# The first RMS norm of x: sum of squares of the second tile on VectorE, both roots before both scalings

## The reference, cut to what matters

```python
def rmsnorm(x, g):
    xf = x.astype(jnp.float32)
    y = xf * lax.rsqrt(jnp.mean(xf * xf, axis=-1, keepdims=True) + EPS)
    return (y * g.astype(jnp.float32)).astype(x.dtype)

h = rmsnorm(x, ln_mix_g)
proj = h @ w_in            # 1024 -> [lru_x | lru_gate | q | k | v]
# ... recurrent branch, attention, output projection, cross-attention,
# ... a mixer over 128*128 experts (most of the time), final norm
```

## Time and profile before

| what | value |
|---|---|
| median of 3 runs | 969.2 us (968.04 to 970.23) |
| the profiled execution | 968.83 us |
| its span in the profile | 967.0 us |
| PE busy | 954.4 us (99%) |
| DVE busy | 806.9 us (83%) |
| ACT busy | 542.6 us (56%) |
| POOL busy | 486.4 us (50%) |

### The profile page before, as it was taken

One profiled execution on the slowest core, in us unless ns is written; L12 is line 12 of the kernel. 1 busy time (PEld: TensorE's weight loads), 2 busy tenths in 40 slices (PEclk: granted clock), 3 DMA queues, 4 the chain that ended last, 5 costly groups with the idle time before them and its releaser, 6 DMA issues.

```text
span 967.0 us, 18013 instructions
## 1 busy us (share of the span) xinstructions
PE 954.4 (99%) x6807; PEld 915.2 (95%) x6807; DVE 806.9 (83%) x1571; ACT 542.6 (56%) x953; POOL 486.4 (50%) x315
## 2 busy tenths in 40 slices
PE   8999999999999999999999999999999999999997
PEld 8897799999999999999998888889999999999997
DVE  5988866446999999999988787777899899999897
ACT  7775546555555546464465565545555455555456
POOL 1001001001488888888788888827478872242210
PEclk9999999999999999999999999999999999999999
DMA  9699865434547787878878878878999999999992
GB/s 317 218 316 323 269 226 200 147 123 139 175 82 203 180 208 179 213 169 205 202 189 208 194 174 194 201 202 307 329 362 345 338 347 374 361 372 354 366 339 95
DMA packets 134265, 235.61 MB, mean 244 GB/s; under 512 B 38624, under 2 KB 87520, under 8 KB 133824
## 3 DMA queue, kind: packets, MB, share of 16 engines
q1 hardware_dynamic: 97552, 208.66, 64.4%
q0 software_dynamic: 36224, 25.70, 14.1%
q10 hardware_dynamic: 432, 0.57, 0.2%
HBM read 216.38 MB, written 17.97 MB: 242 GB/s over the span
## 4 chain that ended last, share of the span: by engine, by line
PE 51%; POOL 33%; issue 8%; DVE 5%; ACT 2%; DMA 1%; ACTq 0%; POOLq 0%; DVEq 0%
POOL wmap L478 33%; PE acc L1702 11%; PE bank L1702 11%; PE acc L1438 11%; PE bank L1703 5%; PE acc L1703 5%; PE acc L1420 3%; DVE wsp L893 1%; PE acc L1421 1%; PE acc L1424 1%; ACT wsp L511 1%; PE bank L1544 1%; PE bank L1391 1%; DMA wmap<-gate,widx 1%; PE bank L1566 1%
## 5 line engine op out<-in xcount | busy, mean ns | idle before, releaser
L478 POOL DMA_INDIRECT wmap<-gate,widx x192 | 322.3, 1679 | 90.8 <-issue 60.0
L762 ACT ACTIVATE hl<-raw 128x1024 fp32r<-128x1024 f32 x192 | 202.3, 1058 | 80.3 <-PE bank L1668 41.7
L1143 DVE TENSOR_TENSOR hl<-raw,hl 128x1024 fp32r<-128x1024 f32 x99 | 120.9, 1221 | 24.2 <-ACT hl L762 24.1
L1635 PE MATMUL bank<-xt,hl 128*128 128x256 f32 x480 | 136.0, 283 | 0.0
L1636 PE MATMUL bank<-xt,hl 128*128 128x256 f32 x480 | 135.9, 283 | 0.0
L1637 PE MATMUL bank<-xt,hl 128*128 128x256 f32 x480 | 135.9, 283 | 0.0
L501 POOL DMA_INDIRECT vg<-v,idx_v x48 | 74.3, 1549 | 119.0 <-DVE acc_s L1284 99.7
L1150 DVE TENSOR_TENSOR hl<-raw,hl 128x512 fp32r<-128x512 f32 x186 | 119.3, 687 | 17.0 <-ACT hl L762 15.8
L1702 PE MATMUL bank<-whl,hl 128*128 128x416 f32 x380 | 121.1, 369 | 0.7 <-DVE acc L1292 0.7
L1702 PE MATMUL acc<-whl,hl 128*128 128x416 f32 x380 | 121.7, 371 | 0.0
L1667 PE MATMUL bank<-xt,hl 128*128 128x512 f32 x288 | 102.4, 399 | 0.0
(11 more groups left out here) (306 smaller groups left out, 2379.6 us busy)
## 6 DMA issues: line engine op xcount, KB each, us to landing
raw<-u_t SPq DMA_DIRECT2D x128, 512.0 KB, 4.5
raw<-v SPq DMA_DIRECT2D x128, 512.0 KB, 5.9
wmap<-zeros SPq DMA_DIRECT2D x6, 2048.0 KB, 11.7
wblk<-wmap SPq DMA_DIRECT2D x62, 192.0 KB, 6.1
wraw<-w_in SPq DMA_DIRECT2D x9, 1024.0 KB, 9.4
wraw<-w_pq SPq DMA_DIRECT2D x8, 1024.0 KB, 5.3
wraw<-w_ck SPq DMA_DIRECT2D x4, 1024.0 KB, 8.4
wraw<-w_cv SPq DMA_DIRECT2D x4, 1024.0 KB, 7.0
```

What stands on the lines that cost most here:

```text
L478: nc.gpsimd.indirect_dma_start(out=wmap, out_offset=bass.IndirectOffsetOnAxis(ap=set_ranks(widx, k)[:, h, r:r + 1], axis=0), in_=set_ranks ...
L762: nc.scalar.activation(eslot(k, 0, second), raw[:, k // 2, k % 2], ACT.Copy).then_inc(ready, 1)
L1143: V.tensor_tensor(eslot(k, 1, second), raw[:, k // 2, k % 2], eslot(k, 0, second).bitcast(F32), ALU.subtract).then_inc(ready, 1)
L1635: pe.matmul(dst, uh[:, c], xt[:, c, 0], start=(c == 0), stop=False)
```

## The change

ScalarE now squares and sums tile 0 alone. VectorE waits for tile 1 of x, squares and sums it itself (a `scalar_tensor_tensor` that computes (x*1)*x and has an accumulator output), then waits until both sums are there, makes both means, and after that does reciprocal and scaling of tile 0 and of tile 1. ScalarE takes both roots one after the other. The norms of other stages keep their order; `tile_norm` is only split into two functions.

```diff
             warm_sqrt()
+            act.wait_ge(s_x[0], 16)
+            squares(0, 0, xr, xs)
             for t in range(TT):
-                act.wait_ge(s_x[t], 16)
-                squares(0, t, xr, xs)
                 tile_deviation(0, t)
...
+                mean_square(n, t)
+                scale_tile(n, t, src, dst)
+
+            def mean_square(n, t):
+                ss = stat[:, SS + 2 * n + t:SS + 2 * n + t + 1]
                 V.tensor_scalar(ss, ss, 1.0 / D, EPS, ALU.mult, ALU.add).then_inc(s_var, 1)
+
+            def scale_tile(n, t, src, dst):
                 dve.wait_ge(s_std, norm_count(n, t))
...
             V.memset(stat[:, WARM:WARM + 1], 1.0).then_inc(s_warm, 1)
+            dve.wait_ge(s_x[1], 16)
+            V.scalar_tensor_tensor(xs[:, 1], xr[:, 1], 1.0, xr[:, 1], ALU.mult, ALU.mult,
+                                   accum_out=stat[:, SS + 1:SS + 2]).then_inc(s_sq, 1)
+            dve.wait_ge(s_sq, TT)
             for t in range(TT):
-                tile_norm(0, t, xr, xs)
+                mean_square(0, t)
+            for t in range(TT):
+                scale_tile(0, t, xr, xs)
```

## The result

| | before | changed |
|---|---|---|
| median, 22 runs each | 968.55 us | 970.78 us |
| lowest to highest | 966.95 to 970.25 | 967.84 to 974.95 |
| profiled execution, its span | 968.83, 967.0 us | 970.91, 969.1 us |

The ratio is 1.0025, with a 95% interval of 1.0014 to 1.0037: the change costs 2.2 us. The forecast was 970.1 us, a loss of 0.9 us, which it took for no change; the time lies in its range, the loss is more than twice the forecast one. The second row of that table already hints at the reason: the lowest of the changed kernel lies 0.9 us above the lowest of before, the highest 4.7 us above.

What follows compares the result with a forecast made beforehand. TensorE, busy for 99% of the span, was taken to bound the kernel, so a first projection 0.9 us later arrives whole at the end: 969.2 + 0.9 = 970.1 us, range 968.6 to 971.9, counted as no change.

Steps and rivals of the forecast that it cites:

- What bounds the kernel: TensorE, busy for 99% of the span: a later first projection shifts all behind it by as much, 0.9 us.
- Steps 1 to 4, the serial tail: First norm: tile 1's sum at 7.14, both scalings in a row on VectorE, second done at 9.39; plus 0.87 us.
- Step 5, TensorE: Tile 0's eight transposes run from 8.56 to 9.49, 0.93 us, and tile 1's follow: plus 0.93 us.
- The rival on the clock: TensorE, idle from 6.84 to 8.56, keeps the slow clock until the first projection: 2.8 us more, 972.9 us; chance 0.06.
- Half rate of the product: VectorE's accumulating product on tile 1 runs at half the rate: 1.22 us more, 971.4 us; chance 0.08.
- Slower by over 0.2%: Whole kernel: the case of a loss above 0.2%, from half rate, slow clock and scatter; chance 0.13.

Runs made afterwards that it cites:

- e5: The changed kernel as it is, run again beside a new set of before: 971.19 us, ratio 1.0022.
- e1: The changed kernel with 14 instead of 10 products on zeros ahead of the first transposes, filling TensorE's gap: 969.53 us, ratio 1.0006.
- e3: The kernel before with only the order changed: ScalarE squares both tiles, then both means, both roots, both scalings: 969.25 us, ratio 1.0014.
- e10: The changed kernel as it is, run again beside the one with 14 products on zeros (e9): 971.20 us, ratio 1.0019.
- e6: The changed kernel with 6 instead of 10 products on zeros, so that TensorE idles longer: 971.98 us, ratio 1.0032.
- e7: The kernel before with ScalarE taking the root straight from its own sum, no VectorE mean for these two tiles: 968.53 us, ratio 1.0002.
- e2: The kernel before with 7 instead of 10 products on zeros, nothing of the change: 969.59 us, ratio 1.0011.
- e9: The changed kernel with 14 instead of 10 products on zeros, as e1, now beside the changed kernel as it is (e10): 969.53 us, ratio 1.0003.

## Why the forecast was right and where it fell short

**The number.** That 970.78 us lies only 0.7 from the forecast 970.1 is partly luck. The forecast stood on 969.2 us, the median of three runs; in 22 runs the kernel before has 968.55. This hides 0.65 us of the 1.3 us by which the loss itself was missed.

**What bounds the kernel.** Right. The start of the expert pass (line 1635 of before, line 1648 now) follows the first projection: 278.2 us before, 280.5 with the change, 278.9 with the gap filled, 281.7 in e5.

```profile
L1635 PE MATMUL bank<-xt,hl x480: 278/283/382, 278.2 to 505.2; 128*128 128x256 f32 x160
```

```profile
L1648 PE MATMUL bank<-xt,hl x480: 278/283/387, 280.5 to 507.5; 128*128 128x256 f32 x160
```

A few tenths are absorbed on the way in some of them (0.88 at the start of e1, 0.7 at 278 us). In e5 the shift grew, from 3.0 at the projection to 3.5, since the projection itself began at the low level. The whole span follows as well in the changed kernel (2.2 us later at the projection, 2.1 us longer), but a single span proves little: e3's was 1.0 us shorter than that of before although its projection began 0.84 us later.

**Steps 1 to 4, the serial tail.** Right, each within about 0.1 us: tile 1 landed at 5.78 (5.8), the product took 1.23 us (1.22) and its read ended at 7.03 (7.14, since the read costs 0.08 us on VectorE and overlaps the product, where I had added 0.10 behind it), the second scaling ended at 9.30 (9.39). The argument that mattered holds: ScalarE was free when tile 1 landed, so moving its squares gains nothing, and e3 shows the same times with the squares on ScalarE. Then both scalings stand in a row on VectorE and tile 0 has lost its slot.

**Step 5, TensorE.** Here the forecast fell short: the waits and their order are right, the price of the transposes is not. It took 0.93 us for eight transposes, their time at the high clock, for the new place too. In the changed kernel's profile 16 took 3.07 us, in e5 and e10 3.65 and 3.37. The two levels are 421 and 273 ns for one transpose.

**The rival on the clock.** The mechanism was written down with its place. Its full price of 3.7 us was a little high: in e5 the projection started 3.0 us late, in e6 3.1 us, since 16 transposes at the low level take 3.44 us (8.63 to 12.07) and not twice 1.86, and at the start of the expert pass the two were 3.5 and 3.0 us late. What was too small is its chance, 0.06. It rested on two readings: that the work up to 6.84 was the same, and that in the trace of before the clock rose with the first transpose. Both are true and neither bears on the question. The first says nothing of what comes after 6.84, and in the changed kernel's profile the clock had risen before the gap, as the shortest of the matmuls on zeros shows (275 ns; the median took 421), and fell behind it:

```profile
L1494 PE MATMUL acc<-zeros x20: 275/421/579, 2.2 to 6.1; 128*128 128x128 f32 x20
```

The second showed how thin the margin was: in that execution of before the clock had not yet risen when the gap began, and 0.35 us later there was work again. It should have been read as a warning. E3 and e5 show that with the same work on TensorE and nearly the same gap one execution finds the high level and another the low one. So the right form of this rival was a mixture with a mean price: about 1.3 us on the medians (2.2 - 0.9), and in single profiles from 0 to 2.1 us at the projection (13.64 - 10.60 - 0.9 in e5), or 2.8 us at the expert pass (281.7 in e5, 278.9 in e1).

**Half rate of the product.** Refuted: 1.23 us with the sum, 1224 ns without it. Of the two readings of the sentence in the Trainium skill (Vector Engine (DVE) Microarchitecture Reference, section 7), the one in which the sum costs more on top is ruled out by this. Whether the product alone is what the page calls half throughput stays open: it takes 1.6 times the 0.75 us of the scaling, not twice.

**Chances.** Slower by over 0.2% had 0.13, and 0.23% to 0.25% was measured (medians and ratio); the interval of 1.0014 to 1.0037 does not exclude either side of the bound. What stays open is how often the low clock occurs in the changed kernel: three of three profiles had it, while four of the 22 runs lay at 967.84 to 968.19 us, 0.9 to 1.2 us above the lowest of before, where an execution without it belongs. E3's profile shows that a gap of 1.71 us need not bring it. The clock doesn't explain the highest runs either: the most that it cost, with the tail, was 3.5 us (e5 at the expert pass), and e5's span was 4.8 us longer than that of before.

## What to carry to other kernels

Before an engine is relieved, look whether it was late at all: here the input of tile 1 landed 0.17 us before its engine took it up, and no division of the squares between engines can start them sooner than that. When two short pipelines are merged into "all of step one, then all of step two", the first tile loses its early slot and whoever consumes it idles; here the later start itself was the smaller part of the bill (0.9 us) and the clock behind the idle time the larger (1.3 us on the medians). After a change that moves TensorE's first real work, filler work in front of it has to be sized anew: four more products on zeros gave back more than half of this loss by the medians. And before an early shift is priced by single spans, look how much the rest of the kernel varies by itself: here a milestone behind the change, the start of the expert pass, told more than the end.

## What the runs showed of the hardware

- VectorE's product with an accumulated sum costs the same as the plain one (1.23 us against 1224 ns for 128x1024 float32), and handing out the sum takes 0.08 us, where ScalarE's takes 0.19.
- A root on 128x1 elements takes ScalarE 0.20 us plain and 0.29 us with a scale and a bias operand from memory (e7).
- The clock can fall while TensorE is working again: in the changed kernel the transposes began at 8.59 and the granted clock fell at about 9.2. The same work and nearly the same gap can end at either level (e3 and e5), so one profile does not settle what a gap costs.
- The scatter of this kernel has a second, separate source: in e3's profile TensorE is busy without a break from 640 to 655 us and the span is 966.0 us although the projection began at 11.44, while in the profile of before it idles there for 0.7 us, waiting for VectorE (DVE acc L1292), and the span is 967.0. From the start of the expert pass to the end it is 687.2 us in e2, e3 and e7, the three profiles without a break in that stretch, and 688.6 to 690.1 in the others, with the change or without it; only e9, with its wait of 4.0 us, has 698.0.

The two rows of that last point are TensorE's table for e3 and a wait of TensorE in the kernel before:

```profile
640.00:655.00 15.00, 15.00 (x94) 1.00 0.61 205
```

```profile
PE bank L1702 <- DVE acc L1292: 0.7, 1, 0.7
```
